# Three edits to a diffusion-transformer step: a conditioning vector partly summed on VectorE, squared relu on ScalarE, a low part computed one split later

## The chip, the core and the metric

The kernel runs on one core of a Trainium2 chip. Its time is the device time of one execution in microseconds (us). Five engines work side by side: TensorE (PE in the profile; PEld is its weight load), VectorE (DVE), ScalarE (ACT), GpSimd (POOL) and SyncE (SP). Here SP issues the loads of the layer weights, and POOL those of the conditioning weights. Engines wait for each other through semaphores, and each works through its own instructions in program order.

## The reference

Two layers of a transformer act on 128 context tokens and 128 latent tokens, 2048 wide. Each layer is modulated by six vectors per token kind, which come from a matrix product with the conditioning input:

```python
mod_ctx = (silu(c_ctx) @ w_ada[l] + b_ada[l])[None, None, :]
mod_lat = (silu(c) @ w_ada[l] + b_ada[l])[:, None, :]
shift1, scale1, gate1, shift2, scale2, gate2 = split(mod, 6)
h = rms_norm(x, g_attn) * (1 + scale1) + shift1
mix = concat(conv_module, global attention, windowed attention)(h @ w_in) @ w_out
x = x + gate1 * mix
h2 = rms_norm(x, g_mlp) * (1 + scale2) + shift2
x = x + gate2 * (square(relu(h2 @ w_mlp1)) @ w_mlp2)
```

w_ada[l] is 2048 x 12288, w_mlp1 2048 x 8192, w_mlp2 8192 x 2048, all float32. At the end both streams are normalised and written, with the keys and values of the context.

## The kernel before

**Pairs, halves, chunks.** Both token kinds lie side by side as 256 columns. A layer is 7 pairs of input projection, 4 of output projection, and 4 chunks c of the MLP with 4 "up" and 4 "down" pairs each. A pair makes 512 output rows in two halves g, each of which fills two PSUM banks from 16 blocks of 128 weight rows. A half is cut into four chunks h of four blocks. TensorE's `pair` (L705) does per block two matmuls of 512 columns with the weight's high part (L727) and two of 256 with its low part (L730).

**The split of the weights.** A weight is written as a rounded high part and the remainder. Per chunk ScalarE's `split_hi` (L965) makes the high part from the raw block, and VectorE's `split_lo` (L1298) the difference. There are four slots of each, so the split of chunk o waits until TensorE has finished chunk o - 4, and in each half both engines go through splits 4g+3 to 4g+6, that is three ahead. I call them splits 3, 4, 5 and 6 for either half. SP loads the raw blocks into four slots.

**The end of a half.** ScalarE copies the low products to `tmp` (`copies`, L1059), VectorE adds the banks to `tsum` (`both_summed`, L1481). In an up half VectorE squares the relu into `thid` (L1443), ScalarE rounds that into `act2` (L1044), and VectorE writes the low part (L1446). Only then does each engine come to the next half's split 3, VectorE to its `split_lo` and ScalarE to its `split_hi`, in this order of program. In a down half VectorE adds four pieces to `xT` (L1500). The next down pairs read `act2`, chunk h from the tiles 4h to 4h + 3; TensorE waits for them by `act2_ready`.

**The conditioning vectors.** Vectors are numbered v = 6 * layer + position. A vector is 16 row blocks k of `w_ada` (128 x 2048, 1 MB each). A unit is one block: four matmuls of 512 columns into four strips of a PSUM bank (`ada_products`, L605). POOL loads the blocks into five slots, `ring`: two in `ada`, two in `ring_q`, one in `thin`. Units stand in TensorE's stream behind chunk h = 2, as `units_inside` (L353) says: vector 4 two a half in the output pairs; vector 5 two behind norm 2, two in the second half of c = 0, then four in every second half, from four slots in turn; vector 6 one a half in c = 1, from slots 1 and 4.

Vectors 7 and 8 are folded instead: VectorE multiplies half a block (128 x 1024, `fold_in`, the slot 0) by the conditioning value of either token kind and adds it to `fold` (`fold_step`, L1463, L1474 for the first block and L1478 for the others), so a load is two steps. At the end TensorE sums the 128 rows of each kind with two units (`fold_sum`, L611). `fold_plan` (L1752) says which half does which loads: none in c = 0 up, then one a half, two in some, and two in every second down half. A fold step stands behind a split's low part. There are two buffers of half a block; POOL issues load n + 2 when both steps of load n are done, and issues a half's fold loads ahead of its unit load.

Of the kernel before, what the change touches and what calls it, by code (L numbers as in the profile page):

```python
# [11 lines left out]
S = 2  # L12
# [37 lines left out]
WIDE_VECTORS = (5, 11)  # L50
THIN_VECTOR = 6
FOLDED = (7, 8)
FOLD_LOADS = 2 * KT
FOLD_STEPS = FOLD_LOADS * S
# [47 lines left out]
def build(nc, t):  # L102
# [124 lines left out]
    relu2_ready, hid_hi = sem("relu2_ready"), sem("hid_hi")  # L227
# [90 lines left out]
    def unit_slot(v, k):  # L318


        if v == THIN_VECTOR:
            return (1, 4)[k % 2]
        if v in WIDE_VECTORS:
            return (k + 2 * (v == WIDE_VECTORS[0])) % 4
        return (0, 1, 4)[k % 3]

    def units_of(v):

        return S if v in FOLDED else KT
# [5 lines left out]
    def slot_uses(v, k):  # L335


        return [(w, j) for w in range(PRE_JOBS // 4, v + 1) if w not in FOLDED for j in range(KT if w < v else k)
                if unit_slot(w, j) == unit_slot(v, k)]
# [95 lines left out]
    with block:  # L435
# [64 lines left out]
        def _(pool):  # L500
# [11 lines left out]
            def thin_load(k):  # L512
                slot = unit_slot(THIN_VECTOR, k)
                pool.wait_ge(ada_used, slot_freed(THIN_VECTOR, k))
                pool.dma_start(ring[slot], w_ada(THIN_VECTOR)[:, k, :]).then_inc(ada_landed[slot], 16)

            def fold_load(load):
                n, at_half = divmod(load, FOLD_LOADS)
                k, h = divmod(at_half, 2)
                if load < 2:  # L520
                    pool.wait_ge(ada_used, used_before(THIN_VECTOR))
                else:
                    pool.wait_ge(folded, S * (load - 1))
                pool.dma_start(fold_in[:, h, :], w_ada(FOLDED[n])[:, k, h * (D // 2):(h + 1) * (D // 2)])\
# [23 lines left out]
            for v in range(PRE_JOBS // 4, THIN_VECTOR):  # L548
                vector(v // VECTORS, v)
            for load in range(2):  # L550
                fold_load(load)
            for k in range(2):
                thin_load(k)
            for c in range(CHUNKS):
                for kind in ("up", "down"):
                    for i in range(UP):
                        for g in range(2):
                            for load in FOLD_AT.get((c, kind, i, g), ()):
                                if load + 2 < FOLD_LOADS * len(FOLDED):
                                    fold_load(load + 2)  # L560
                            if c == 1 and half_of(kind, i, g) + 2 < KT:
                                thin_load(half_of(kind, i, g) + 2)
            pool.wait_ge(folded, FOLD_STEPS * len(FOLDED))
# [5 lines left out]
        def _(pe):  # L569
# [24 lines left out]
            def ada_unit(l, m, k):  # L594
# [4 lines left out]
                if v in FOLDED:  # L599
                    fold_sum(v, k)  # L600
                    return
                pe.wait_ge(ada_landed[unit_slot(v, k)], 16 * units_landed(v, k))
                ada_products(k, ring[unit_slot(v, k)])

            def ada_products(k, unit):  # L605
# [1233 lines left out]
```

## Time and profile before

| | us |
|---|---|
| median of 3 runs | 2247.67 (2246.96 to 2249.29) |
| the profiled execution | 2247.72 |
| its span, first to last instruction | 2245.9 |
| TensorE busy | 2200.5 |
| VectorE busy | 1523.4 |
| ScalarE busy | 1081.0 |

Busy times are sums over the whole span, and they do not tell which engine sets the pace of a stage; that is to be read from the timeline of the stage. A row of a timeline is the start, the duration, the engine and line, the operation, and in brackets how long the engine was idle before it and what it waited for. The bracket is left out where there was no idle time.

### The profile page before, as it was taken

How to read it: one execution, taken by the hardware profiler on the slowest of the kernel's cores; microseconds unless marked ns; L12 is line 12 of the kernel's file. 1: busy time of each engine (PE TensorE's matmuls, PEld its weight loads, DVE VectorE, ACT ScalarE, POOL GpSimd, SP SyncE). 2: the span in 40 equal slices, each digit the busy share in tenths (PEclk: the TensorE clock that was granted, in tenths of full speed). 3: DMA queues.
4: the chain of work that ended last, by engine and by line, in shares of the span. 5: the costliest groups of instructions: out<-in, count | busy, mean ns of one | idle time of the engine just before them, and what ended most of it. 6: DMA issues, size and time to landing. Idle time of an engine off the chain costs nothing.

```text
span 2245.9 us, 33331 instructions
## 1 busy us (share of the span) xinstructions
PE 2200.5 (98%) x13310; PEld 1823.1 (81%) x13310; DVE 1523.4 (68%) x2218; ACT 1081.0 (48%) x1566; POOL 112.4 (5%) x217
## 2 busy tenths in 40 slices
PE   6899999999999999999999999999999999999998
PEld 3677787778887888888887787888788888888887
DVE  2378765757877868888867876675556656655665
ACT  2245664644444334444455557574344444444444
POOL 1000100000000100000000000000000000000000
PEclk8999999999999999999999999999999999999999
DMA  9998878888888977887767787568756565556652
GB/s 374 407 381 323 297 275 318 291 308 296 264 282 297 333 231 236 265 255 230 230 232 261 285 322 259 203 202 281 243 188 182 192 192 188 191 190 189 192 190 95
DMA packets 403145, 571.07 MB, mean 254 GB/s; under 512 B 10744, under 2 KB 356976, under 8 KB 386352
## 3 DMA queue, kind: packets, MB, share of 16 engines
q1 hardware_dynamic: 372368, 398.77, 53.6%
q0 software_dynamic: 28320, 168.08, 19.9%
q8 instruction: 106, 1.74, 0.3%
q10 hardware_dynamic: 2304, 2.10, 0.3%
q14 instruction: 47, 0.39, 0.0%
HBM read 565.76 MB, written 3.15 MB: 253 GB/s over the span
## 4 chain that ended last, share of the span: by engine, by line
PE 94%; SPq 2%; DMA 2%; DVE 2%; ACT 1%; issue 0%; ACTq 0%; DVEq 0%
PE bank L727 46%; PE bank L730 22%; PE bank L823 9%; PE bank L607 5%; PE bank L826 4%; SPq L452 1%; PE bank L653 1%; PE bank L763 1%; DMA ada<-in_w_ada 1%; DVE lo L1302 1%; DMA raw<-in_w_in 1%; PE bank L629 1%; PE bank L766 1%; PE bank L656 0%; ACT hi L970 0%; PE bank L922 0%
## 5 line engine op out<-in xcount | busy, mean ns | idle before, releaser
L1302 DVE TENSOR_TENSOR lo<-raw,hi 128x1024 fp32r<-128x1024 f32 x688 | 833.0, 1222 | 334.8 <-ACT hi L970 333.4
L970 ACT ACTIVATE hi<-raw 128x1024 fp32r<-128x1024 f32 x688 | 716.2, 1055 | 568.9 <-PE bank L730 430.2
L727 PE MATMUL bank<-act,hi 128*128 128x512 f32 x2304 | 725.5, 396 | 0.5 <-DVE tsum L1486 0.5
L727 PE MATMUL bank<-hs,hi 128*128 128x512 f32 x2048 | 646.9, 397 | 0.2
L730 PEld LDWEIGHTS bank<-act,lo 128*128 128x128 f32 x2304 | 432.8, 188 | 102.4
L730 PEld LDWEIGHTS bank<-hs,lo 128*128 128x128 f32 x2048 | 385.0, 188 | 91.1
L730 PE MATMUL bank<-act,lo 128*128 128x256 f32 x2304 | 452.7, 278 | 0.0
L730 PE MATMUL bank<-hs,lo 128*128 128x256 f32 x2048 | 402.6, 278 | 0.0
L727 PEld LDWEIGHTS bank<-act,hi 128*128 128x128 f32 x2304 | 350.7, 189 | 12.4 <-DVE lo L1302 6.7
L727 PEld LDWEIGHTS bank<-hs,hi 128*128 128x128 f32 x2048 | 311.8, 189 | 18.7 <-issue 17.2
L1061 ACT ACTIVATE tmp<-bank 128x512 f32<-128x512 f32 x164 | 98.0, 597 | 345.3 <-PE bank L730 274.4
L823 PE MATMUL bank<-hs,hi 128*128 128x512 f32 x768 | 247.4, 403 | 0.1
L1486 DVE TENSOR_TENSOR tsum<-bank,tmp 128x512 f32<-128x512 f32 x140 | 96.7, 690 | 193.5 <-ACT tmp L1061 193.4
L826 PEld LDWEIGHTS bank<-hs,lo 128*128 128x128 f32 x768 | 144.4, 188 | 34.2
L1478 DVE SCALAR_TENSOR_TENSOR ring_q<-ada,cT,ring_q 128x1024 f32<-128x1024 f32 x120 | 153.4, 1279 | 0.0
L826 PE MATMUL bank<-hs,lo 128*128 128x256 f32 x768 | 151.3, 278 | 0.0
L823 PEld LDWEIGHTS bank<-hs,hi 128*128 128x128 f32 x768 | 117.5, 189 | 14.8 <-issue 10.4
L1614 DVE SCALAR_TENSOR_TENSOR yconv<-hpad,vecs,yconv 128x256 f32<-128x256 f32 x240 | 100.5, 478 | 0.0
L1044 ACT ACTIVATE act<-thid 128x512 fp32r<-128x512 f32 x64 | 40.4, 631 | 110.2 <-DVE thid L1443 110.2
L1500 DVE SCALAR_TENSOR_TENSOR xT<-tsum,mods,xT 128x128 f32<-128x128 f32 x304 | 86.6, 347 | 2.7
L607 PE MATMUL bank<-ada,cT 128*32 128x512 f32 x632 | 82.6, 617 | 1.0 <-DVE mods L1309 1.0
L1446 DVE TENSOR_TENSOR act<-thid,act 128x512 fp32r<-128x512 f32 x64 | 44.4, 693 | 53.5 <-ACT act L1044 53.5
(190 smaller groups left out, 1374.9 us busy)
## 6 DMA issues: line engine op xcount, KB each, us to landing
raw<-in_w_mlp SPq DMA_DIRECT2D x256, 1024.0 KB, 5.8
ada<-in_w_ada POOLq DMA_DIRECT2D x79, 1024.0 KB, 7.5
raw<-in_w_in SPq DMA_DIRECT2D x56, 1024.0 KB, 6.5
thin<-in_w_ada POOLq DMA_DIRECT2D x33, 1024.0 KB, 7.2
raw<-in_w_out SPq DMA_DIRECT2D x32, 1024.0 KB, 5.4
ada<-in_w_ada POOLq DMA_DIRECT2D x64, 512.0 KB, 4.3
pre_a<-in_w_ada SPq DMA_DIRECT2D x32, 512.0 KB, 10.8
ring_q<-in_w_ada POOLq DMA_DIRECT2D x16, 1024.0 KB, 9.8
```

Of the source, the lines that this page charges most:

```text
L607: mm = pe.matmul(ada_ps[32 * q:32 * q + 32, :], cT[:, k, :], unit[:, q * 512:(q + 1) * 512], start=(k == 0), stop=(k == KT - 1))
L727: pe.matmul(pb[2 * g + j][:, :], hi[:, h, k, j * P:(j + 1) * P], acts[:, k_, :], start=(k_ == 0), stop=False)
L730: mm = pe.matmul(pb[2 * g + j][:, TOK:2 * TOK], lo[:, h, k, j * P:(j + 1) * P], acts[:, k_, 0:TOK], start=False, stop=(k_ == KT - 1))
L823: pe.matmul(pb[2 * g + j][:, :], hi[:, slot, k, j * P:(j + 1) * P], acts[:, 4 * x + k, :], start=start, stop=False)
L826: mm = pe.matmul(pb[2 * g + j][:, TOK:2 * TOK], lo[:, slot, k, j * P:(j + 1) * P], acts[:, 4 * x + k, 0:TOK], start=False, stop=stop)
L970: act.activation(hi[:, o % 4, :, :], raw_chunk(n, o, s, sub), ACT.Copy).then_inc(hi_ready, 1)
L1061: act.activation(tmp[:, :, :], psum[:, 2 * g:2 * g + 2, TOK:2 * TOK], ACT.Copy).then_inc(tmp_ready, 2)
L1302: dve.tensor_tensor(lo[:, o % 4, :, :], raw_chunk(n, o, s, sub), hi[:, o % 4, :, :].bitcast(f32), ALU.subtract).then_inc(lo_ready, 1)
L1478: dve.scalar_tensor_tensor(fold[:, s, cols], fold_in[:, h, :], cT[:, k, s:s + 1], fold[:, s, cols], ALU.mult, ALU.add).then_inc(folded, 1)
L1486: dve.tensor_tensor(tsum[:, :, :], psum[:, 2 * g:2 * g + 2, 0:TOK], tmp[:, :, :], ALU.add)\
L1500: dve.scalar_tensor_tensor(x, total[:, :, s * P:(s + 1) * P], mods[:, l, bass.ds(gate + 4 * i + 2 * g + j, 1), s], x, ALU.mult, ALU.add).t ...
L1614: dve.scalar_tensor_tensor(y, hpad[:, ch, :, tap:tap + P], vecs[:, l, 1, 4 * tap + ch:4 * tap + ch + 1], y, ALU.mult, ALU.add).then_inc(co ...
```

## The change

- Vector 5 (`UP_VECTOR`) is done in pairs of units, in each up half of c = 0 but the first, from the slots 1 and 4 alone.
- Vector 6 (`SHARED_VECTOR`): blocks 0 to 7 stay units, in pairs in halves 8, 9, 11 and 12; blocks 8 to 15 are folded by VectorE in halves 1 to 7 and summed by two units in half 10.
- Vectors 7 and 8 are folded in halves 11 to 34 and 36 to 59, one load a half and two in every third.
- In an up half ScalarE does the relu, from `tsum` to `tmp`, and the square, from `tmp` to `thid`; VectorE's product is gone, and its next sum waits until the relu has read `tsum`.
- The low part of the squared relu is written by `hidden_lo`, in the next half, behind split 3 and the fold steps of that place.
- POOL's order in a half: that half's fold loads, then two unit loads.

```diff
+UP_VECTOR = 5
+SHARED_VECTOR = 6
+SHARED_TILES = 8
+FOLD_FIRST = {6: SHARED_TILES, 7: 0, 8: 0}
...
-        if v == THIN_VECTOR:
+        if v in (UP_VECTOR, SHARED_VECTOR):
             return (1, 4)[k % 2]
...
     def units_of(v):
-        return S if v in FOLDED else KT
+        return S if v in FOLDED else SHARED_TILES + S if v == SHARED_VECTOR else KT
+
+    def summed_part(v, k):
+        if v in FOLDED:
+            return k
+        return k - SHARED_UNITS if v == SHARED_VECTOR and SHARED_UNITS <= k < SHARED_UNITS + S else None
...
+        if a is not None and l == 0:
+            return [(a // 4, 4 * i + 2 * g + u) for u in range(0 if follows_norm(kind, i, c) and g == 0 else 2)]
         if a is not None and g == 1:
             return [(a // 4, 4 * i + u) for u in range(2 if follows_norm(kind, i, c) else 0, 4)]
-        if l == 0 and c == 1:
-            return [(THIN_VECTOR, half_of(kind, i, g))]
-        if l == 0 and (c, kind, i, g) in FOLD_SUMS:
-            return [(FOLD_SUMS[c, kind, i, g], s) for s in range(S)]
+        half = 2 * UP * 2 * c + half_of(kind, i, g)
+        if l == 0 and 0 <= half - SHARED_AT < (SHARED_TILES + S) // 2:
+            return [(SHARED_VECTOR, 2 * (half - SHARED_AT) + u) for u in range(2)]
+        if l == 0 and half in FOLD_SUMS:
+            return [(FOLD_SUMS[half], s) for s in range(S)]
...
+    def half_before(l, kind, i, c, g):
+        if g or i:
+            return kind, i - (g == 0), c, 1 - g
+        return ("up", UP - 1, c, 1) if kind == "down" else ("down", DOWN - 1, c - 1, 1)
...
+            ahead = [(UP_VECTOR, k) for k in range(2, KT)]
+            ahead += [(SHARED_VECTOR, k) for k in range(SHARED_TILES + S) if summed_part(SHARED_VECTOR, k) is None]
+            for half in range(4 * UP * CHUNKS):
+                for load in FOLD_AT.get(half, ()):
+                    if load + 2 < len(FOLD_PLACE):
+                        fold_load(load + 2)
+                for u in range(2):
+                    if ahead:
+                        unit_load(*ahead.pop(0))
...
                         if kind == "up":
                             first = 4 * i + 2 * g
+                            act.wait_ge(bank_freed, 4 * n + 2 * g + 2 - sums_left_out(l, kind))
+                            act.activation(tmp[:, :, :], tsum[:, :, :], ACT.Relu).then_inc(rectified, 2)
+                            act.wait_ge(rectified, up_tiles(l, c) + first + 2)
+                            if first:
+                                act.wait_ge(act2_ready, hidden_base(l, c) + first)
+                            act.activation(thid[:, :, :], tmp[:, :, :], ACT.Square).then_inc(relu2_ready, 2)
                             act.wait_ge(relu2_ready, up_tiles(l, c) + first + 2)
                             act.activation(act2[:, first:first + 2, 0:TOK], thid[:, :, :], ACT.Copy).then_inc(hid_hi, 2)
...
                                 split_lo(n, o)
-                            if l == 0 and (o - 4 * g - 3) // S < len(FOLD_AT.get((c, kind, i, g), ())):
-                                fold_step(FOLD_AT[c, kind, i, g][(o - 4 * g - 3) // S], (o - 4 * g - 3) % S)
+                            if l == 0 and kind != "out":
+                                for load, s in fold_steps(4 * UP * c + half_of(kind, i, g), o - 4 * g - 3):
+                                    fold_step(load, s)
+                            if o == 4 * g + 3:
+                                hidden_lo(*half_before(l, kind, i, c, g))
...
-                        if kind == "up":
-                            dve.scalar_tensor_tensor(thid[:, :, :], tsum[:, :, :], 0.0, tsum[:, :, :],
-                                                     ALU.max, ALU.mult).then_inc(relu2_ready, 2)
-                            dve.wait_ge(hid_hi, up_tiles(l, c) + first + 2)
-                            dve.tensor_tensor(act2[:, first:first + 2, TOK:2 * TOK], thid[:, :, :],
-                                              act2[:, first:first + 2, 0:TOK].bitcast(f32), ALU.subtract)\
-                               .then_inc(act2_ready, 2)
...
+                def hidden_lo(kind, i, c, g, l=l):
+                    if kind == "up":
+                        first = 4 * i + 2 * g
+                        dve.wait_ge(hid_hi, up_tiles(l, c) + first + 2)
+                        dve.tensor_tensor(act2[:, first:first + 2, TOK:2 * TOK], thid[:, :, :],
+                                          act2[:, first:first + 2, 0:TOK].bitcast(f32), ALU.subtract)\
+                           .then_inc(act2_ready, 2)
...
+                    if rectified_before:
+                        dve.wait_ge(rectified, rectified_before)
...
 def fold_plan():
+    at = {1: 3, 2: 3}
+    at.update({half: 2 for half in range(3, 8)})
+    for half in range(11, 35):
+        at[half] = 2 if half % 3 == 2 else 1
+    for half in range(36, 60):
+        at[half] = 2 if half % 3 == 0 else 1
     plan, first = {}, 0
+    for half in sorted(at):
+        plan[half] = range(first, first + at[half])
+        first += at[half]
...
+def fold_steps(half, position):
+    steps = [(load, s) for load in FOLD_AT.get(half, ()) for s in range(S)]
+    return steps[position::4] if len(steps) < 4 else steps[position * len(steps) // 4:(position + 1) * len(steps) // 4]
...
+FOLD_SUMS = {35: FOLDED[0], 61: FOLDED[1]}
```

In the diff halves are numbered through layer 0: 16c + position, up halves before down halves.

## Rows read from the trace of the kernel before

**Rows 1.** The page: TensorE's busy time, and the chain's shares by engine.
```profile
PE 2200.5 (98%) x13310; PEld 1823.1 (81%) x13310; DVE 1523.4 (68%) x2218; ACT 1081.0 (48%) x1566; POOL 112.4 (5%) x217
...
PE 94%; SPq 2%; DMA 2%; DVE 2%; ACT 1%; issue 0%; ACTq 0%; DVEq 0%
```

**Rows 2.** TensorE's waits: engine, line, awaited work, us in total, times, longest.
```profile
PE bank L653 <- DVE lo L1302: 6.0, 1, 6.0
```

**Rows 3.** Timeline of POOL: start, us, engine, line, operation, idle time before.
```profile
359.63 0.53 POOL L510 DMA_DIRECT2D ada<-in_w_ada  x1 [11.83 <-PE bank L607]
...
372.85 0.53 POOL L510 DMA_DIRECT2D thin<-in_w_ada  x1 [11.83 <-PE bank L607]
...
651.01 0.53 POOL L524 DMA_DIRECT2D ada<-in_w_ada  x1 [11.16 <-DVE ring_q L1478]
...
663.35 0.53 POOL L524 DMA_DIRECT2D ada<-in_w_ada  x1 [11.16 <-DVE ring_q L1478]
...
1050.56 0.53 POOL L524 DMA_DIRECT2D ada<-in_w_ada  x1 [10.61 <-DVE ring_q L1478]
```

**Rows 4.** Pieces of the chain that ended last: start, us, what.
```profile
444.18 1.85 PE bank L607 x16
468.55 3.57 PE bank L607 x32
494.61 3.57 PE bank L607 x32
```

**Rows 5.** Timeline of VectorE, an up half and the half behind it.
```profile
716.79 0.69 DVE L1486 TENSOR_TENSOR tsum<-bank,tmp 128x512 f32<-128x512 f32 x1 [2.11 <-ACT tmp L1061]
717.60 0.69 DVE L1443 SCALAR_TENSOR_TENSOR thid<-tsum 128x512 f32<-128x512 f32 x1
...
720.00 1.23 DVE L1302 TENSOR_TENSOR lo<-raw,hi 128x1024 fp32r<-128x1024 f32 x1 [0.19 <-ACT hi L970]
721.14 1.28 DVE L1478 SCALAR_TENSOR_TENSOR ring_q<-ada,cT,ring_q 128x1024 f32<-128x1024 f32 x1
722.34 1.22 DVE L1302 TENSOR_TENSOR lo<-raw,hi 128x1024 fp32r<-128x1024 f32 x1
...
729.33 0.68 DVE L1486 TENSOR_TENSOR tsum<-bank,tmp 128x512 f32<-128x512 f32 x1
```

**Rows 6.** Timeline of VectorE, a fold step on a vector's first block.
```profile
833.97 0.75 DVE L1474 TENSOR_SCALAR ring_q<-ada,cT 128x1024 f32<-128x1024 f32 x1
```

**Rows 7.** Timeline of ScalarE, the same half, and two operations of a mixer.
```profile
164.70 0.62 ACT L1215 ACTIVATE qsq<-zq 128x512 f32<-128x512 f32 x1
165.35 0.72 ACT L1220 ACTIVATE zq<-zq,vecs 128x512 f32<-128x512 f32 x1
...
716.10 0.60 ACT L1061 ACTIVATE tmp<-bank 128x512 f32<-128x512 f32 x1 [2.91 <-PE bank L730]
718.38 0.63 ACT L1044 ACTIVATE act<-thid 128x512 fp32r<-128x512 f32 x1 [1.69 <-DVE thid L1443]
718.92 1.99 ACT L970 ACTIVATE hi<-raw 128x1024 fp32r<-128x1024 f32 x2
```

**Rows 8.** Four loads in a row, issue to landing; and what the queues moved then.
```profile
DMA to landing us min/median/max: 6.9/9.8/12.9
...
DMA packets 364, 2.43 MB, mean 404 GB/s; under 512 B 32, under 2 KB 73, under 8 KB 73
```

**Rows 9.** Timeline of VectorE, the first up half's sum.
```profile
437.67 0.68 DVE L1486 TENSOR_TENSOR tsum<-bank,tmp 128x512 f32<-128x512 f32 x1
```

**Rows 10.** DMA issues of the page: the fold loads, median us to landing.
```profile
ada<-in_w_ada POOLq DMA_DIRECT2D x64, 512.0 KB, 4.3
```

**Rows 11.** Stretches: busy us of each engine, granted clock, DMA share, GB/s.
```profile
1180.00:1184.00 4.00, 3.02 (x16) 2.05 (x20) 2.11 (x5) 0.85 (x4) 0.00 (x0) 0.58 0.58 195
1184.00:1187.00 3.00, 3.00 (x17) 0.68 (x10) 3.00 (x12) 3.00 (x11) 0.56 (x2) 0.50 0.86 250
```

**Rows 12.** ScalarE's groups by form: table loads at the line of exp.
```profile
L1249 ACT ACT_TABLE_LOAD x6 | 7.7, 1283 | 0.1
```

More of the change, by code:

```diff
@@ L335, in slot_uses @@
     def slot_uses(v, k):
-        return [(w, j) for w in range(PRE_JOBS // 4, v + 1) if w not in FOLDED for j in range(KT if w < v else k)
-                if unit_slot(w, j) == unit_slot(v, k)]
+        return [(w, j) for w in range(PRE_JOBS // 4, v + 1) for j in range(units_of(w) if w < v else k)
+                if summed_part(w, j) is None and unit_slot(w, j) == unit_slot(v, k)]
     def slot_freed(v, k):
@@ L547, in _ @@
                          t["sink"].rearrange("l h -> (l h)").partition_broadcast(P)).then_inc(sinks_in, 16)
-            for v in range(PRE_JOBS // 4, THIN_VECTOR):
+            for v in range(PRE_JOBS // 4, UP_VECTOR):
                 vector(v // VECTORS, v)
+            for k in range(2):
+                unit_load(UP_VECTOR, k)
             for load in range(2):
                 fold_load(load)
[L552 to L563, printed above, removed]
+            ahead = [(UP_VECTOR, k) for k in range(2, KT)]
[7 more added lines that the diff above has]
+                        unit_load(*ahead.pop(0))
+            pool.wait_ge(folded, S * len(FOLD_PLACE))
             for v in range(FOLDED[-1] + 1, DEPTH * VECTORS):
@@ L598, in ada_unit, with ada_products @@
                 v = l * VECTORS + m
[L599 to L605, printed above, removed]
-                for q in range(4):
-                    mm = pe.matmul(ada_ps[32 * q:32 * q + 32, :], cT[:, k, :], unit[:, q * 512:(q + 1) * 512],
-                                   start=(k == 0), stop=(k == KT - 1))
-                mm.then_inc(ada_used, 1)
-            def fold_sum(v, s):
-                pe.wait_ge(pick_set, 1 + S)
-                pe.wait_ge(folded, FOLD_STEPS * (FOLDED.index(v) + 1))
-                for q in range(4):
-                    mm = pe.matmul(ada_ps[32 * q:32 * q + 32, :], pick[:, s, :], fold[:, s, q * 512:(q + 1) * 512],
-                                   start=(s == 0), stop=(s == S - 1))
+                s = summed_part(v, k)
+                if s is None:
+                    pe.wait_ge(ada_landed[unit_slot(v, k)], 16 * units_landed(v, k))
+                    ada_products(v, k, cT[:, block_of(v, k), :], ring[unit_slot(v, k)])
+                else:
+                    pe.wait_ge(pick_set, 1 + S)
+                    pe.wait_ge(folded, S * FOLD_END[v])
+                    ada_products(v, k, pick[:, s, :], fold[:, s, :])
+            def ada_products(v, k, weights, unit):
+                for q in range(4):
+                    mm = pe.matmul(ada_ps[32 * q:32 * q + 32, :], weights, unit[:, q * 512:(q + 1) * 512],
+                                   start=(k == 0), stop=(k == units_of(v) - 1))
                 mm.then_inc(ada_used, 1)
@@ L1531, in mixers @@
                     for g in range(2):
-                        both_summed("out", n, g)
+                        both_summed("out", n, g, up_tiles(l, 0))
                         for j in range(2):
@@ L1749, in half_of @@
     return 2 * UP * (kind == "down") + 2 * i + g
+FOLD_PLACE = [(v, k, h) for v in (SHARED_VECTOR,) + FOLDED for k in range(FOLD_FIRST[v], KT) for h in range(2)]
+FOLD_END = {v: max(load for load, place in enumerate(FOLD_PLACE) if place[0] == v) + 1 for v in (SHARED_VECTOR,) + FOLDED}
+SHARED_AT, SHARED_UNITS = 8, 4
 def fold_plan():
-    plan, first = {}, 0
-    for c in range(CHUNKS):
-        for kind in ("up", "down"):
-            for half in range(2 * UP):
-                i, g = divmod(half, 2)
-                loads = 1 + (kind == "down" and c < CHUNKS - 1 and g == 0)
-                if kind == "up" and (c == 0 or c == 2 and half < 2):
-                    loads = 2 * g * (c == 2)
-                if kind == "down" and c == CHUNKS - 1 and i > 1:
-                    loads = 0
-                if loads:
-                    plan[c, kind, i, g] = range(first, first + loads)
-                first += loads
-    assert first == FOLD_LOADS * len(FOLDED)
-    return plan
+    at = {1: 3, 2: 3}
[4 more added lines that the diff above has]
+        at[half] = 2 if half % 3 == 0 else 1
+    plan, first = {}, 0
+    for half in sorted(at):
+        plan[half] = range(first, first + at[half])
+        first += at[half]
+    assert first == len(FOLD_PLACE)
+    return plan
+def fold_steps(half, position):
+    steps = [(load, s) for load in FOLD_AT.get(half, ()) for s in range(S)]
+    return steps[position::4] if len(steps) < 4 else steps[position * len(steps) // 4:(position + 1) * len(steps) // 4]
 FOLD_AT = fold_plan()
-FOLD_SUMS = {(2, "up", 0, 0): FOLDED[0], (3, "down", 2, 0): FOLDED[1]}
+FOLD_SUMS = {35: FOLDED[0], 61: FOLDED[1]}
 HEAD_GROUPS = (0, 1, 2, 3, 4, 5, 6, 8, 10)
```

48 lines of the change are left out of this document (23 added, 25 removed).

## The prediction

> **What bounds the kernel now.** I read the page's busy shares first, then the chain of waits, then TensorE's own waits. TensorE is busy 98% of the span, and the chain that ends last runs through it for 94% [rows 1]. Its longest wait for VectorE is one of 6.0 us in the opening [rows 2]; in the multi-layer-perceptron part (MLP) its halves of a weight pair keep the length that their matmuls need (below). So two things count: how much TensorE has to do, and whether VectorE, which writes the low parts that TensorE waits for, still keeps up.
>
> I count in halves: half h = 16c + position, 0 to 63 in layer 0; 0-7, 16-23, 32-39 and 48-55 are "up" halves. A half has four chunks (0 to 3) of 2.79 us; vector units stand between chunk 2 and chunk 3. POOL's issues give the period: 0.53 + 10.61 = 11.14 us with no unit (11.15 in what follows), 12.34 with one, 13.22 with two [rows 3]. Two pieces of the chain, four units and then a half with none, lie 26.06 apart [rows 4]: minus 2 x 11.15, four units cost 3.76. So one costs 1.19, two 2.07, four 3.76: 0.86 each and 0.33 per interruption.
>
> **What goes from TensorE.** Before: vector 5 inside the up halves is 1 x 2 and 3 x 4 units, 2.07 + 11.28 = 13.35 us; vector 6 is 16 single ones, 19.04; together 32.4. After: seven pairs and five pairs (the two sums of the folded rows count as units), 12 x 2.07 = 24.8. Saved: 7.6 us, all on the path. The sums move from halves 32 and 60 to 35 and 61 at the same price.
>
> **What VectorE gets.** 16 more loads of half a block, two fold steps each: 32 steps in halves 1 to 7; later vectors are spread anew, with two loads (4 steps) in every third half instead of in "down" halves. The question is how long VectorE needs for one up half when it runs late. The trace has such a half: from one tsum at 716.79 to the next at 729.33, with four fold steps and no idle time before the second, 12.54 us [rows 5]. A fold step adds 1.20 to it (721.14 to 722.34). The first block of a vector is a plain multiply, 0.75 instead of 1.28 long [rows 6]: 0.53 less.
>
> Now the edits of the relu. Before, from tsum's start to the low part of split 3 is 720.00 - 716.79 = 3.21 us, and two VectorE operations of 0.69 stand in it. After, ScalarE does relu, square and copy there, and its split 3 is queued behind the copy, by its program order; so VectorE can do nothing until all of it is through. Price: tsum 0.69, release 0.09 (thid ends 718.29, ScalarE starts 718.38), relu 0.62 and its wait 0.03 (164.70 to 165.35, a square of the same size and the next operation, which waits for it), square 0.65, then 0.54 from the copy's start to the split's, and 1.08 to the low part [rows 5, 7]: 3.70. The deferred low part adds 0.61 behind it (its spacing, 0.69 less the overlap). Cycle with four steps: 12.54 - 3.21 + 3.70 + 0.61 = 13.65; with two 11.25, with six 16.05, with none 8.85. Against it TensorE's half: 11.15, or 13.2 with a pair of units. So each 4-step half puts VectorE 2.5 us further behind where there are no units, and 0.45 where there are. The move to ScalarE takes 0.7 us of work from VectorE and gives 3.1 us of idle time: it makes the cycle 1.1 longer. The bounds of the 3.70: 3.2 (ScalarE as fast as VectorE's own chain was) and 4.3 (each of three waits 0.2). In layer 1, with no fold steps, 8.85 is under 11.15 and costs nothing. At a change from up to down, TensorE's chunk 3 needs the deferred part: ready 0.8 + 5.6 = 6.4 us into the half with no steps, needed at 8.36; hidden, 2 us of cover.
>
> The Trainium skill ("ScalarE: Activation LUTs", Rules for kernel authors) says to put relu on VectorE. The trace agrees that it is the dearer place: 0.69 against 2 x 0.62 and a wait of 0.03, 0.6 more. Taken as a loss in each of the 64 up halves that would be 38 us, and 2278; by the rows it costs only where VectorE is late, and the sum below goes by that.
>
> **When TensorE stops.** Let S be the start of a half's first tsum (0.8 after the last half's end E if VectorE is on time: 716.10 for tmp, 716.79 for tsum [rows 5, 7]) and B = S + cycle. Then E >= S + 5.0 + 2.8 (low part of split 3, then chunk 3), the next chunk 0 not before S + 7.9, and the next S = max(E + 0.8, B). In a half behind the last up half, E >= S + 9.6 (deferred part). VectorE may be some 2.3 us late for free.
> c=1, halves 16 to 24, steps 2,4,2,2,4,2,2,4,2, from E = 0: S = 0.8, 12.05, 25.7, 36.95, 48.2, 61.85, 73.1, 84.35, 98.0; E of the last 107.6 against 9 x 11.15 = 100.35: 7.2 us of stalls, mostly in 21 (2.4) and 24 (4.2).
> c=2, 32 to 40: half 35 has no steps and two units, and lets VectorE catch up; 36 has cheap first steps (11.5). E 104.9 against 102.4: 2.5.
> c=3, 48 to 56, steps 4,2,2,4,2,2,4,2,2: again 7.2.
> Sum 16.9. With both ends of the 3.70 the cycle moves by -0.5 or +0.6 a half: 9 and 29.
>
> **The pairs of units in c=0.** POOL issues the two loads of the next pair behind the last fold load of the half, and that waits for the half's last fold step, at B. Vector 5 has now only two buffers, so nothing is ahead. Four loads in a row landed 6.9 to 12.9 us after their issues, 0.53 apart: the first after 6.9, each further one (12.9 + 1.59 - 6.9)/3 = 2.5 later [rows 8]. So from the fold load: 0.53 + 6.9 + 2.5 = 9.9, then the second unit 0.86, restart 0.4, chunk 3 2.8: E = B(last half) + 14.0, or E + 13.2 if that is later. VectorE starts half 1 late already (437.67; the unit piece at 444.18 less three chunks puts the half's start at 435.8): S = 1.9 [rows 4, 9]. Half 1 has six steps, four of them cheap, and its third load lands 1.2 late (issued after the first one's second step, 4.3 to land [rows 10]).
> Halves 1 to 7: B = 17.0, 33.05, 46.7, 61.5, 75.15, 89.95, 103.6; E of 1 to 8 = 13.2, 31.0, 47.05, 60.7, 75.5, 89.15, 103.95, 117.6 against 8 x 13.2 = 105.6: 12.0 us. Bounds: loads that land 1 us sooner or later give 6 and 18. The bytes: 5.24 MB a half (raw 2.1, units 2.1, folds 1.05), in 13.2 us 397 GB/s, where the busiest stretch moved 404 [rows 8]; no slack, but no term of its own.
>
> **Clock.** After a stretch with TensorE busy 3.02 of 4 us the granted clock was 0.50 (the 1.2 GHz level) for 3 us [rows 11]. A stall of over 2 us may bring this on, 1.5 us each, some eight times; most fall where VectorE is the bound anyway. I take 2, ends 0 and 12.
>
> **Sum.** -7.6 + 16.9 + 12.0 + 2 = +23.3 on the profiled execution's 2247.7 us (span 2245.9, and 1.8 around it), which is the median of the runs shown: 2271.
>
> **Rivals.**
> A. All stalls stay hidden (VectorE's lag is taken up by the four-deep splits, the loads land in time): 2247.7 - 7.6 = 2240. For it: in the kernel before, a 4-step half after an up half cost nothing. Against it: its cycle was 12.54 beside 12.34, the new one 13.65 beside 11.15. Chance 0.16.
> B. Only the pairs' loads are late: a VectorE cycle of 12.4 gives B = E, so E grows by 14.0 a half, 0.8 x 7, and some 2 more in each 6-step half: about 9; 2247.7 - 7.6 + 9 = 2249, no change. For it: half 1 to 7 are the only place where a load has one half to land. Chance 0.10.
> C. The loads land in time and VectorE alone holds: then c=0 costs 4 (chunk 3 >= S + 5 with S = 33.05 in half 3, slowly more to half 8), 2247.7 - 7.6 + 4 + 16.9 = 2261. Chance 0.12. It is inside my range.
> D. Relu and copy don't share ScalarE's tables: a load of 1.28 [rows 12] before and after, in each of 64 up halves. On the 24 folding ones of c=1 to 3 that is 2.6 us each, some 60 us on top: 2330. Against it: the trace has loads at the lines of exp, sqrt and sigmoid, and none between a square and a copy. Chance 0.02. The Trainium skill ("ScalarE: Activation LUTs", Table sets: the hidden batching unit) says that relu and copy are in every set; by that rule D cannot be, and the sum stays.
> The forecast itself 0.60, own range 2255 to 2284.
>
> **How the numbers follow.** What a measurement here can tell from no change is 0.2%, 4.5 us. Faster: A, 0.16. Within: B, 0.10. Slower: forecast, C and D, 0.74. The range goes from 2246 (leaves A out) to 2284 (bounds of the three costs, not all at once).
>
> **What would show it.** Right: tsum in the 4-step halves with no idle time before it, VectorE idle about 3.1 us before the low part of split 3 in each up half, TensorE waiting for the low part in halves 18 to 24 and 49 to 56 and for ada or thin in 2 to 7; the vectors' 128x512 matmuls down from 1040 to 1016. Wrong: VectorE idle before tsum in halves 20 and 23, or POOL's pair loads issued before the half's end in c=0. If TensorE's waits in the MLP are under 5 us in all, rival A holds.

## The result, and the profile after

The changed kernel takes 2285.3 us (median of 4 runs, 2280.9 to 2288.1) against 2247.7 of the kernel before (4 runs, 2247.0 to 2249.3): ratio 1.0165, 95% interval 1.0153 to 1.0177. It is slower, as forecast, but by 37.6 us where 23.3 were forecast, and 1.3 us above the range. The profiled execution is the fastest of the four: 2280.9, span 2279.1.

The page after. TensorE has 48 instructions fewer than in [rows 1] (six units, 8 records each) and yet 7.7 us more busy time; its share of the chain fell from 94% to 86%.

```profile
PE 2208.2 (97%) x13262; PEld 1829.1 (80%) x13262; DVE 1504.9 (66%) x2186; ACT 1158.3 (51%) x1694; POOL 117.1 (5%) x225
...
PE 86%; DMA 4%; DVE 4%; issue 2%; ACT 2%; SPq 2%; POOL 0%; ACTq 0%; DVEq 0%
```

TensorE's waits between 430 and 1240 us (awaited work, us in total, times, longest). Beside the 6.0 of [rows 2], which lies in the opening and is still there, the kernel before had none of the first four:

```profile
PE bank L737 <- DVE act L1499: 7.0, 3, 3.3
PE bank L627 <- DMA ada<-in_w_ada: 6.2, 3, 3.5
PE bank L627 <- DMA thin<-in_w_ada: 6.1, 5, 1.7
PE bank L737 <- DVE lo L1318: 5.9, 4, 2.3
PE bank L596 <- ACT thid L1083: 0.9, 2, 0.6
```

VectorE's timeline after, an up half with two fold steps (from the first sum to the second) and one with four; it answers to [rows 5].

```profile
686.64 0.68 DVE L1510 TENSOR_TENSOR tsum<-bank,tmp 128x512 f32<-128x512 f32 x1
690.54 1.23 DVE L1318 TENSOR_TENSOR lo<-raw,hi 128x1024 fp32r<-128x1024 f32 x1 [3.22 <-ACT hi L980]
...
692.88 0.69 DVE L1499 TENSOR_TENSOR act<-thid,act 128x512 fp32r<-128x512 f32 x1
...
698.09 0.69 DVE L1510 TENSOR_TENSOR tsum<-bank,tmp 128x512 f32<-128x512 f32 x1
701.99 1.23 DVE L1318 TENSOR_TENSOR lo<-raw,hi 128x1024 fp32r<-128x1024 f32 x1 [3.22 <-ACT hi L980]
...
711.93 0.68 DVE L1510 TENSOR_TENSOR tsum<-bank,tmp 128x512 f32<-128x512 f32 x1
```

No idle time stands before the sums: VectorE is the bound, with 11.45 us from sum to sum (686.64 to 698.09) and 13.84 (to 711.93). In both VectorE sits idle for 3.22 us behind its sum, until ScalarE's high part is there: 3.90 us from the sum's start to the low part. Why is in ScalarE's timeline of the same place; it answers to [rows 7].

```profile
698.87 0.63 ACT L1054 ACTIVATE tmp<-tsum 128x512 f32<-128x512 f32 x1 [3.30 <-DVE tsum L1510]
699.58 0.63 ACT L1058 ACTIVATE thid<-tmp 128x512 f32<-128x512 f32 x1
700.31 0.63 ACT L1060 ACTIVATE act<-thid 128x512 fp32r<-128x512 f32 x1
700.85 3.89 ACT L980 ACTIVATE hi<-raw 128x1024 fp32r<-128x1024 f32 x4
```

In chunk 0 of the MLP the pairs' loads come first. TensorE in half 2 waits for both; the two loads were issued behind the fold load of 453.90 (POOL's timeline, then TensorE's):

```profile
453.90 0.53 POOL L541 DMA_DIRECT2D ada<-in_w_ada  x1 [4.76 <-issue]
454.42 0.53 POOL L533 DMA_DIRECT2D ada<-in_w_ada  x1
454.94 0.53 POOL L533 DMA_DIRECT2D thin<-in_w_ada  x1
```

```profile
460.79 1.94 PE L627 MATMUL bank<-ada,cT 128*32 128x512 f32 x8 [3.53 <-DMA ada<-in_w_ada]
463.46 1.94 PE L627 MATMUL bank<-thin,cT 128*32 128x512 f32 x8 [0.74 <-DMA thin<-in_w_ada]
465.33 1.22 PE L737 MATMUL bank<-hs,hi 128*128 128x512 f32 x2
```

A unit takes 1.94 there, where at 480.29 it takes 1.07. The reason is the granted clock (third number from the end of a row; the same view as [rows 11]), at the 1.2 GHz level from 460 to 468:

```profile
456.00:460.00 4.00, 1.26 (x8) 0.92 (x6) 3.81 (x4) 2.94 (x4) 0.00 (x0) 0.91 1.01 414
460.00:464.00 4.00, 2.48 (x12) 0.40 (x16) 4.00 (x5) 0.00 (x0) 0.53 (x1) 0.50 0.97 347
464.00:468.00 4.00, 4.00 (x16) 2.29 (x9) 2.21 (x2) 0.00 (x0) 0.53 (x1) 0.50 0.99 334
```

ScalarE's table loads are those of [rows 12], at exp, sqrt and sigmoid, and none at the relu:

```profile
L1265 ACT ACT_TABLE_LOAD x6 | 7.7, 1283 | 0.1
```

**Where the time went.** I compare the profiles by ScalarE's first operation at the end of each half (`tmp`), in four stretches, one for each chunk c: halves 1 to 8, 16 to 24, 32 to 40 and 47 to 56. They take 106.55, 100.32, 103.28 and 111.46 us when TensorE never stops (back_best, the last version of the table below; what lies between the stretches is equal to 0.3 us in all kernels with the new plan). The table gives the excess over these, the excess of halves 1 to 62 as a whole ("sum", so up to 0.3 beyond its four columns), and TensorE's idle time there in waits of over 0.25 us:

| kernel | median us | c=0 | c=1 | c=2 | c=3 | sum | idle |
|---|---|---|---|---|---|---|---|
| after | 2285.3 | 19.9 | 10.6 | 3.3 | 7.1 | 40.8 | 25.2 |
| relu_back | 2257.5 | 11.2 | 0 | 0 | 0 | 11.2 | 7.7 |
| units_first | 2277.7 | 11.1 | 11.4 | 4.6 | 7.0 | 34.4 | 20.3 |
| hi_first | 2253.2 | 8.0 | 0 | 0 | 0 | 8.0 | 4.7 |
| no_relu | 2266.7 | 16.5 | 4.5 | 1.2 | 1.6 | 23.7 | 16.5 |
| slots | 2282.0 | 16.6 | 11.3 | 5.7 | 7.0 | 40.9 | 27.2 |
| best | 2241.2 | 0.5 | 0 | 0 | 0 | 0.5 | 0 |
| best_no_hi | 2267.5 | 5.4 | 10.5 | 3.3 | 7.0 | 26.2 | 17.6 |
| best_folds_first | 2243.4 | 7.7 | 0 | 0 | 0 | 7.7 | 5.1 |
| best_no_even | 2252.7 | 13.3 | 0 | 0 | 0 | 13.3 | 8.6 |
| back_best | 2240.4 | 0 | 0 | 0 | 0 | 0 | 0 |

From the end of half 0 to that of half 62 the kernel before takes 731.2 us, back_best 723.6: the 7.6 of the forecast. With 40.8 on top the changed kernel is at 764.4, 33.2 more than before, and so is its profiled execution (2280.9 against 2247.7). The columns say that idle time is not all: 40.8 us were lost to 25.2 of it.

### The profile page after: what moved, and what is told of

It is laid out like the page before. It is cut to its first block, busy times and chain, and to the rows that moved or that the text cites. A ratio compares the mean times of both kernels' runs of the same rounds, so it can differ in the third digit from the quotient of the medians.

```text
span 2279.1 us, 33485 instructions
## 1 busy us (share of the span) xinstructions
PE 2208.2 (97%) x13262; PEld 1829.1 (80%) x13262; DVE 1504.9 (66%) x2186; ACT 1158.3 (51%) x1694; POOL 117.1 (5%) x225
## 4 chain that ended last, share of the span: by engine, by line
PE 86%; DMA 4%; DVE 4%; issue 2%; ACT 2%; SPq 2%; POOL 0%; ACTq 0%; DVEq 0%
PE bank L737 41%; PE bank L740 20%; PE bank L833 9%; PE bank L627 5%; PE bank L836 4%; DMA thin<-in_w_ada 2%; DVE lo L1318 2%; SPq L470 2%; DVE ring_q L1491 1%; DMA ada<-in_w_ada 1%; DMA raw<-in_w_in 1%; PE bank L773 1%; ACT hi L980 1%; PE bank L663 1%; PE bank L776 1%
## 5 line engine op out<-in xcount | busy, mean ns | idle before, releaser
L1491 DVE SCALAR_TENSOR_TENSOR ring_q<-ada,cT,ring_q 128x1024 f32<-128x1024 f32 x148 | 189.2, 1280 | 6.7 <-DMA ada<-in_w_ada 6.7
L1054 ACT ACTIVATE tmp<-tsum 128x512 f32<-128x512 f32 x64 | 40.5, 633 | 102.0 <-DVE tsum L1510 102.0
L541 POOL DMA_DIRECT2D ada<-in_w_ada x80 | 42.4, 530 | 621.7 <-DVE ring_q L1491 546.1
```

Of the source, the lines that this page charges most:

```text
L1491: dve.scalar_tensor_tensor(fold[:, s, cols], fold_in[:, h, :], cT[:, k, s:s + 1], fold[:, s, cols], ALU.mult, ALU.add).then_inc(folded, 1)
```

## The experiments

Beside them the kernel before took 2247.7 to 2248.7 us (medians). The diffs are shortened: dots stand for code left out, and long lines are abridged.

**relu_back.** The changed kernel with the three relu edits undone, loads and fold plan as changed.

```diff
-act.activation(tmp, tsum, ACT.Relu); act.activation(thid, tmp, ACT.Square)
-if o == 4 * g + 3: hidden_lo(*half_before(...))
+dve.scalar_tensor_tensor(thid, tsum, 0.0, tsum, ALU.max, ALU.mult); hidden_lo(kind, i, c, g)
```

> The changed kernel with the relu's three edits undone: relu and square in one VectorE operation, its low part at once, before the next half's split 3. The fold plan and the pairs stay. Theory 1 (VectorE's cycle of an up half grew to 13.8 us because it stands idle while ScalarE does relu, square and copy ahead of split 3): the cycle goes back to 12.5 with four steps and 10.2 with two, the stalls in c=1 to 3 (20.9 us in the changed kernel) vanish, those in c=0 (20.8) fall to about 11; 2252 to 2258. Theory 2 (it is the amount of VectorE's work in the up halves, 32 more fold steps, and the relu's edits relieve it): 0.7 us more work per up half, so no faster than 2285.

2257.5 (2254.0 to 2264.2), ratio 1.005 (1.0034 to 1.0065). All stalls of c=1 to 3 are gone. c=0 keeps 11.2 us: 7.7 us of waits, all for loads, and the rest behind them, most of it at the 1.2 GHz level in half 2. So the three relu edits together cost 28 us of the 38.

**relu_only.** The other half: the kernel before with the three relu edits, its own vectors and fold plan.

> The kernel before with the three edits of the relu alone (relu and square on ScalarE, low part behind split 3); its fold plan, thin units and groups of four stay. Theory 1: a cycle with two steps is 11.45 against TensorE's 11.15 in c=2 and c=3 up, so the lag grows by 0.3 a half and ends in a stall of 1.5 to 2 us at the change to down, twice: 2250 to 2252, slower by 0.1 to 0.2%. Theory 2 (less work for VectorE is a relief): 2247 or faster, and no stall.

2253.0 (2250.6 to 2254.1), ratio 1.0021 (1.0012 to 1.003), 1 us above what the first theory gave. The edits alone cost 5 us, in two places (halves 40 and 56, behind the last up half of c=2 and c=3):

```profile
PE bank L733 <- DVE act L1493: 3.5, 2, 2.0
```

5 us alone and 28 with the new fold plan: they matter by what VectorE still has to do in up halves. The kernel before has no fold step in those of c=0 and two in most of the others; the changed one has four or six in c=0, and elsewhere four in every third half and two in the rest.

**units_first.** The changed kernel, POOL issuing the two unit loads of a half ahead of its fold loads.

```diff
 for half in range(4 * UP * CHUNKS):
+    for u in range(2): ... unit_load(*ahead.pop(0))
     for load in FOLD_AT.get(half, ()): ... fold_load(load + 2)
-    for u in range(2): ... unit_load(*ahead.pop(0))
```

> The changed kernel with one order turned: in each half POOL issues the two unit loads ahead of that half's fold loads, so they wait for TensorE's units and no longer for VectorE's last fold step. Theory 1: the waits of TensorE for ada and thin in halves 2 to 8 vanish, the lag of VectorE stays; c=0 stalls fall from 20.8 to 5 to 9, the rest stays: 2269 to 2275. Theory 3 (the transfers themselves are the bound in c=0, 397 GB/s asked of 404): no gain, 2283 or more.

2277.7 (2273.6 to 2282.9), ratio 1.0132 (1.0114 to 1.0151), above the 2269 to 2275 of the first theory and below the 2283 of the other. No wait for ada or thin is left in the MLP of layer 0, so the transfers do fit. VectorE's lag takes over in c=0: six waits for `lo`, 7.2 us, where the changed kernel had none, and 11.1 us of excess where 5 to 9 were expected. Two limits lay there on top of each other.

**hi_first.** The changed kernel, ScalarE making the high part of split 3 ahead of the relu. All else on ScalarE and VectorE stays.

```diff
+ahead = o == 4 * g + 3 and half_before(l, kind, i, c, g)[0] == "up"
+if not (last and o >= 8 or o == 3 and follows_norm(kind, i, c) or ahead): split_hi(n, o)
 ...
 first = 4 * i + 2 * g
+split_hi(*((n + 1, 3) if g else (n, 7)))
 act.wait_ge(bank_freed, ...)
 act.activation(tmp[:, :, :], tsum[:, :, :], ACT.Relu).then_inc(rectified, 2)
```

> The changed kernel with ScalarE's order turned in an up half: the high part of the next half's split 3 comes right behind the copy of tmp, ahead of relu, square and copy. All the work stays on its engine. Theory 1: VectorE's idle 3.2 us before split 3's low part goes, the cycle is about 10.9 with four steps and 13.4 with six, under TensorE's half; stalls in c=1 to 3 vanish (-20.9), those in c=0 fall to 5 to 8: 2248 to 2254. Theory 2 (the amount of work): nothing changes, 2285.

2253.2 (2247.4 to 2257.1), ratio 1.0023 (1.0013 to 1.0032). One instruction three places further ahead in its queue removes all stalls of c=1 to 3. Here is VectorE with it, in the best version below, at a place like that of the timeline above:

```profile
687.48 0.69 DVE L1517 TENSOR_TENSOR tsum<-bank,tmp 128x512 f32<-128x512 f32 x1
688.43 1.23 DVE L1325 TENSOR_TENSOR lo<-raw,hi 128x1024 fp32r<-128x1024 f32 x1 [0.27 <-ACT hi L985]
...
698.62 0.69 DVE L1517 TENSOR_TENSOR tsum<-bank,tmp 128x512 f32<-128x512 f32 x1 [1.14 <-ACT tmp L1084]
```

0.27 us of idle time behind the sum instead of 3.22, and now the sum waits for `tmp`, i.e. for TensorE.

**no_relu.** The changed kernel without the relu; ScalarE's chain is one operation shorter, the order stays.

> The changed kernel without the relu itself: ScalarE squares tsum directly, so its chain between tsum and its high part of split 3 is one operation (0.71 us) shorter; everything else, order and loads included, stays. It leaves the relu out of the computation. T1 (the length of ScalarE's chain sets VectorE's cycle, and the cycle sets the stalls): cycle of a 4-step up half 13.1 instead of 13.84, of a 2-step one 10.7 instead of 11.45. By the same recursion as in the prediction the last up half of chunks 1 and 3 then ends 3.5 us late instead of 7.2; measured with the slow clock behind it, chunks 1 to 3 should lose 7 to 12 us together instead of 20.8, chunk 0 (halves 0 to 8) 3 to 6 less than the 20.8 of the changed kernel. Time 2266 to 2273. T2 (not the length but the crossing of queues costs, ScalarE's high parts behind anything of VectorE's): the stalls stay above 17 us in chunks 1 to 3, time over 2278.

2266.7 (2262.6 to 2269.5), ratio 1.0087 (1.0072 to 1.0102). The cycle of a 4-step half is 13.11 (692.17 to 705.28), and c=1 to 3 lose 7.3 us instead of 20.9: both as worked out from the length of the chain. 0.7 us off each cycle is worth 18.6 us of the whole, the slow clock behind the stalls included.

**slots.** The changed kernel with the first four units of vector 5 there before half 0 (the first two in the buffers 2 and 3).

> The changed kernel with vector 5's first four units already there at half 0: its first two go to ring buffers 2 and 3 (free since the mixers), the next two to buffers 1 and 4. T1 (the wait for thin at norm 2 and a part of the waits of half 2 come from only two buffers being ahead): no wait for thin before half 0, half 0 starts at 436 or before in each run (the changed kernel's median loses 2 to 4 us there, its profiled run 1.2), and half 2 (21.4 us with 8.2 of stall) gets 2 to 5 shorter; the VectorE part stays, 20.8 us in chunks 1 to 3. Time 2275 to 2281. T2 (half 2 is set by VectorE and the late fold load, not by the pair's loads): halves 0 to 8 stay within 1.5 us of 126.4; time 2281 to 2285.

2282.0 (2276.4 to 2283.2), ratio 1.0151 (1.0136 to 1.0166), 1 us above the first theory's 2275 to 2281. A wait of 1.2 us at norm 2 has gone, but half 2 is only 0.95 us shorter (20.42) where 2 to 5 were expected: two more buffers do not help while each pair is issued behind VectorE's last fold step. That wait I had not foreseen. The kernel before has four buffers there; in the changed one POOL sends vector 5's second unit only when `thin` is free of vector 4, at 412.32, and TensorE wants it at norm 2, ahead of half 0 (POOL's timeline, then TensorE's wait between 400 and 437 us):

```profile
412.32 0.53 POOL L533 DMA_DIRECT2D thin<-in_w_ada  x1 [11.54 <-PE bank L627]
```

```profile
PE bank L627 <- DMA thin<-in_w_ada: 1.2, 1, 1.2
```

It is 1.2 us in the profiled execution of the changed kernel, and 0.9, 2.2, 3.7 and 4.6 in those of no_relu, units_first, hi_first and relu_back, which run the same code up to that place. So it seems to vary from run to run; no kernel was profiled twice.

**best.** hi_first and units_first together, two fold loads in each of halves 1 to 8, and the buffers of slots.

```diff
-    at = {1: 3, 2: 3}
-    at.update({half: 2 for half in range(3, 8)})
+    at = {half: 2 for half in range(1, 9)}
```

> The changed kernel with four edits: ScalarE's high part of split 3 ahead of the relu; POOL issues a half's two unit loads ahead of its fold loads; two fold loads in each of halves 1 to 8 instead of three in 1 and 2; the first four units of vector 5 loaded before half 0. T1 (ScalarE's order, the load order and the two buffers are all that costs; the saving of 7.6 us by pairs is real): halves 0 to 8 in 105.6 to 108, chunks 1 to 3 at 100.35, 103.3 and 111.5, time 2238 to 2244, faster than both kernels. T2 (VectorE's four fold steps a half don't fit into the 13.2 us of a half with a pair, whatever the order): halves 0 to 8 stay over 112, time 2247 or more. T3 (the transfers don't fit, 397 GB/s asked for): waits for ada and thin over 5 us between halves 1 and 8, time over 2246.

2241.2 (2239.1 to 2241.8, 8 runs), ratio 0.997 (0.9959 to 0.998): faster than both. TensorE's waits of over 0.25 us in halves 1 to 62 are gone, at 382 GB/s between 440 and 560 us.

**back_best.** The same loads and plan with the relu on VectorE as before.

> The changed kernel with the relu back on VectorE in the order of the kernel before, and the three edits of the loads (unit loads ahead of fold loads, two fold loads in each of halves 1 to 8, the first four units of vector 5 loaded before half 0). T1 (pairs and folding are worth 7.6 us, and only their load order took it away): halves 0 to 8 in 105.6 to 108, time 2238 to 2244. Beside the version with ScalarE's relu and the high part ahead it tells what the relu's place is worth by itself: by T1 nothing, within 2 us. T2 (with VectorE's full load a 4-step half takes 12.54, under 13.2, but the relu on ScalarE is needed for slack): over 3 us slower than that version.

2240.4 (2239.1 to 2241.7, 8 runs), the same interval. The place of the relu is worth nothing by itself: all of the gain is the six units and eight interruptions (22 groups of units in halves 1 to 62 before, 14 after) that TensorE is spared.

**best_no_hi, best_folds_first, best_no_even.** One edit of the best version put back in each. The fourth, the buffers of slots, was not put back by itself.

> The best version (2241.2 us) with only its ScalarE order put back: high part of split 3 behind relu, square and copy again, the three load edits stay. T1 (that order alone sets VectorE's cycle of 13.84 in a 4-step half; loads are no part of it): chunks 1 to 3 lose 20 to 22 us again; in chunk 0, four steps in every half, the cycle is 0.6 over the 13.2 us of a half with a pair, seven halves, 4 us of lag of which 2 are free, and the last fold half passes into one with none: 2 to 7 us. Time 2263 to 2270. T2 (load order and ScalarE order each were a half of it): below 2255.

> The best version with only its load order put back: POOL issues a half's fold loads ahead of its two unit loads again. T1 (a pair behind the last fold load arrives about E + 13.2 or a little later, so TensorE waits a little in each of the halves 2 to 8; with VectorE on time B = E + 0 and 14.0 - 13.2 = 0.8 a half): halves 0 to 8 in 110 to 113 instead of 107.0, chunks 1 to 3 as in the best version, time 2243 to 2248. T2 (with four units ahead and VectorE on time the order is free): within 1 us of the best version.

> The best version with only the fold plan put back: three fold loads (six steps) in halves 1 and 2, two in 3 to 7, none in 8. T1 (a six-step half takes VectorE 2.4 us longer than the 13.2 of a half with a pair, twice, with the third load 1.2 late; about 2.3 us are free, so some 2 to 5 us are lost and with them perhaps 1.5 by the clock): halves 0 to 8 in 109 to 114, time 2243 to 2248. T2 (the splits ahead hide it): within 1 us of the best version.

2267.5, 2243.4 and 2252.7: ScalarE's order costs 26.3, the load order 2.2 and the uneven fold plan 11.5. The first two times came as worked out, though in the profiled execution of best_folds_first, at 2246.5 one of its slowest, halves 0 to 8 took 114.3 where at most 113 were expected. The third cost is two to five times what I expected, and the timelines of VectorE and POOL show why:

```profile
462.29 2.48 DVE L1498 SCALAR_TENSOR_TENSOR ring_q<-ada,cT,ring_q 128x1024 f32<-128x1024 f32 x2 [15.30 <-DMA ada<-in_w_ada]
464.69 0.68 DVE L1517 TENSOR_TENSOR tsum<-bank,tmp 128x512 f32<-128x512 f32 x1
```

```profile
445.50 0.53 POOL L538 DMA_DIRECT2D ada<-in_w_ada  x1 [30.63 <-PE bank L632]
446.48 0.53 POOL L538 DMA_DIRECT2D thin<-in_w_ada  x1 [0.46 <-PE bank L632]
448.15 1.05 POOL L546 DMA_DIRECT2D ada<-in_w_ada  x2 [1.14 <-issue]
```

The half's third fold load, the first of the two of 448.15, stands in POOL's queue behind the pair, which waits for TensorE's units until 445.50; its own buffer was free from about 443.4. The two half-size loads of 448.15 landed 14.5 us (median) after their issue, and VectorE, whose sum stands behind that fold step in its queue, was idle for 15.3 us. The pair itself took longer than in best, 13.0 and 14.5 us against 9.6 and 11.3; why is open. The pair first is right only where no fold step of the same half still needs a load.

**stall_dose.** What a stall costs, by itself: back_best, and in eight halves TensorE waits ahead of chunk 3 for POOL, which clears a free buffer.

```diff
+if half in DOSES:
+    pool.wait_ge(half_used, 8 * n + 4 * (half % 2) + 3)
+    for m in range(DOSES[half]): ... pool.memset(ring[4][:, 0:512], 0.0).then_inc(dosed, 1)
 ...
+if half in DOSES: pe.wait_ge(dosed, sum(DOSES[x] for x in DOSES if x <= half))
```

> The price of a stall of TensorE measured by itself: the version with VectorE's relu and the three load edits (no stalls of its own in chunks 1 to 3, 2240.4 us), and in eight halves of layer 0 (18, 22, 27, 30, 40, 44, 52, 56) TensorE waits ahead of chunk 3 for POOL, which clears a free buffer 2, 3, 4, 6, 5, 8, 12 and 1 times, one after the other, once chunk 2 is through. Nothing else waits for POOL. T1 (a stall costs its own length and then a stretch at the 1.2 GHz level): after waits of up to about 1 us the periods return at once (excess = wait); after waits of 1.5 us and more the granted clock falls to 0.50 for some us and the excess is 1 to 2.5 us more than the wait; in all the extra is what the changed kernel lost beyond my terms. T2 (a stall costs just its length; the extra us of the changed kernel came from its loads and queues): excess within 0.3 us of the wait in all eight, clock at 0.95 or more. If a clearing takes 0.5 us, the eight waits are 20 us and the time 2260 by T2, 2265 to 2273 by T1.

2293.9 (2 runs), far above both theories' times, 2260 and 2265 to 2273. POOL came to its clearings late, so the eight stalls were longer than planned, 2.5 to 9.7 us and 36.5 in all instead of 20. What they tell is read from each stall:

| half | 27 | 56 | 22 | 30 | 18 | 44 | 40 | 52 |
|---|---|---|---|---|---|---|---|---|
| TensorE idle, us | 2.48 | 2.53 | 3.54 | 3.64 | 4.20 | 4.80 | 5.59 | 9.67 |
| excess of the half and the next, us | 2.71 | 4.32 | 6.33 | 5.18 | 6.01 | 6.60 | 7.72 | 12.47 |
| difference | 0.2 | 1.8 | 2.8 | 1.5 | 1.8 | 1.8 | 2.1 | 2.8 |

TensorE's timeline after the first two of these stalls. The profile names VectorE's low part for the one of half 27, as that ended last (775.70), but POOL's last clearing ended at 775.61, 0.15 us before the matmul, and in half 56 it ended 0.14 before (1136.57), so this is the planned stall too.

```profile
775.76 0.70 PE L753 MATMUL bank<-act,hi 128*128 128x512 f32 x2 [2.48 <-DVE lo L1328]
776.53 0.63 PE L753 MATMUL bank<-act,hi 128*128 128x512 f32 x2
...
1136.71 1.14 PE L753 MATMUL bank<-act,hi 128*128 128x512 f32 x2 [2.53 <-POOL thin L590]
1138.08 1.05 PE L753 MATMUL bank<-act,hi 128*128 128x512 f32 x2
1139.37 1.00 PE L753 MATMUL bank<-act,hi 128*128 128x512 f32 x2
1140.44 0.63 PE L753 MATMUL bank<-act,hi 128*128 128x512 f32 x2
```

Two stalls of one length: after the one a pair of matmuls takes 0.63 at once, after the other 1.05 for some 3.5 us. After the one of half 18 the granted clock was:

```profile
664.00:667.00 3.00, 2.18 (x9) 1.92 (x10) 1.01 (x1) 0.00 (x0) 0.62 (x2) 0.79 0.90 286
667.00:669.00 2.00, 2.00 (x7) 1.61 (x7) 0.00 (x0) 0.00 (x0) 0.00 (x0) 0.50 0.99 323
669.00:672.00 3.00, 3.00 (x19) 2.65 (x18) 1.39 (x2) 0.81 (x2) 0.00 (x0) 0.98 0.09 30
```

So the first theory holds but for half 27, where it expected a slow stretch: a stall costs its length and then either 0.2 us, or 1.5 to 2.8 with a stretch at the 1.2 GHz level, and the second price hardly grows with the length (9.67 us of stall pays 2.8, as 3.54 does).

## Why the prediction missed, by its own steps

**What goes from TensorE (7.6): right.** From half 0 to half 62 it is 731.2 us before against 723.6 in back_best. The count of matmuls that I named as a sign was wrong: the vectors' groups go from 1056 to 1008 records, not from 1040 to 1016.

**VectorE's cycle: right in its cause, 0.2 short in size.** 13.65 and 11.25 were forecast, 13.84 and 11.45 measured. I spaced ScalarE's dependent operations 0.65 apart, as a square and the operation behind it in [rows 7]; relu, square and copy come 0.71 to 0.73 apart (698.87, 699.58, 700.31). Hence 3.90 instead of 3.70. hi_first and no_relu show the cause: the same operations in another order cost nothing, and a chain 0.7 shorter costs a third. Without the clock's part the lag costs 19.1 us where 16.9 were forecast: 8.8 in c=1, 7.0 in c=3 (both from slots, which had no slow clock in c=3 and one in c=1, whose 2.5 are taken off) and 3.3 in c=2.

**The pairs' loads in c=0 (12.0): right within the error.** The excess is 19.9. slots and no_relu, which kept the 2.4 GHz level in halves 4 and 6, had 16.6 and 16.5, so 3.3 of it are two slow stretches. Half 2 has another, 3.9 beyond its idle time; that leaves 12.7. This 3.9 rests on an argument: no kernel had waits of over 3 us in half 2 without a slow stretch. But one part of it I had put elsewhere: the pair came 11.1 us after VectorE's sum (452.30 to 463.4) instead of 9.9, and later halves less. And waits for loads were only the visible limit: units_first took them away, and VectorE's lag kept 11.1 us, 2.5 of them beyond the stall in a slow stretch of half 2.

**The clock (2, ends 0 and 12): this is the step that failed.** I had put it at eight stretches of 1.5 us and took only 2 of these 12, because "most fall where VectorE is the bound anyway". There were six slow stretches (halves 2, 4, 6, 21, 24, 55), each 1.6 to 3.9 us beyond the stall, 12.6 together, and of these 33.2 - (-7.6 + 19.1 + 12.7) = 9.0 us stayed in the time of the profiled execution. So price and number were near, and the share that another engine's lag absorbs was not. The 9.0 is what the other terms leave over, not a measurement of its own; stall_dose measured the price of a stretch. For the stalls in the midst of the up halves my reason holds: in c=3 half 55 had its slow stretch in the changed kernel (4.24 us of excess) and not in slots (2.70), and half 56 paid the rest in idle time, 0.59 against 1.95; both stretches end at 7.0 or 7.1. It does not hold for a stall at the end of VectorE's lag (half 24, 1.8 us) nor in c=0, where slow matmuls follow a wait for a load and the next pair is not nearer for it. My own bound of 12 held it; the value I took was near the other end. [Rows 11] I had read wrongly as well: there the clock fell within the first of the two stretches, at 1180.6, and stayed at the 1.2 GHz level for 6.8 us, not 3. Here is the stall of half 21, first in the changed kernel and then in slots, each with the stretch of 3 us that begins some 2 us behind it:

```profile
717.10 0.73 PE L737 MATMUL bank<-hs,hi 128*128 128x512 f32 x2 [2.25 <-DVE lo L1318]
719.00:722.00 3.00, 3.00 (x11) 2.51 (x10) 3.00 (x3) 0.57 (x1) 0.00 (x0) 0.50 0.90 282
```

```profile
714.10 0.73 PE L742 MATMUL bank<-hs,hi 128*128 128x512 f32 x2 [2.25 <-DVE lo L1323]
716.00:719.00 3.00, 3.00 (x18) 2.54 (x17) 3.00 (x3) 0.60 (x1) 0.41 (x1) 1.00 0.90 286
```

The Trainium skill ("TensorE: Matmul & The Clock Gate", Part 1: The HAM clock gate) says that the clock follows how busy the array was lately and has only two levels, and that the point at which it changes differs from run to run of one kernel. All fourteen traces agree on the levels: the granted clock is 0.50 or 1.00 in each of their records. On the last point they only fit: the stall of half 21, 2.25 us long in four kernels, brought 1.2 GHz in three and not in the fourth, but no kernel was profiled twice.

**The sum.** -7.6 + 19.1 + 12.7 + 9.0 = +33.2 for the profiled execution, against +23.3: +7.0 by the clock, +2.2 by the cycle, +0.7 by the loads. A last part is not in that execution: the median of the runs is 4.4 above it. The wait at norm 2, for which the forecast had no term (1.2 us there, 0.9 to 4.6 in the four other profiles named above), and stretches that are slow in one run and not in the next can make such a difference; slots, without that wait, has a median 3.3 lower. Which share is whose was not separated, so the cause of these 4.4 us, without which the median would have stayed inside the range, is open.

**The rivals.** A (all hidden) and B (only the loads) fall by the waits for `lo` and `act`. C held in part: VectorE alone costs c=0 some 11 us with its slow stretch, and 8.6 without, not 4 (units_first). D falls: no table load stands at the relu.

## What to carry to other kernels

Ask of every instruction that moves to another engine what is queued behind it there: the relu itself was free on either engine, but the high part behind it cost 26 us, and three places further ahead in the queue made it nothing. Load in the order in which the data are needed, and give work that shares a queue in equal portions, or the third load of one half stops two engines. And price a stall of TensorE as its own length plus what a stretch at the slow clock behind it may cost, 1.5 to 3.0 us in these traces, unless another engine's lag absorbs it.

## What the runs showed of the hardware

- Stalls of TensorE in layer 0's MLP that had no other stall within 8 us, counted over all profiled kernels (the granted clock fell within 5 us of their end, or during them): of those under 1.2 us none had the 1.2 GHz level behind it; of 1.3 to 2.0 us, 2 of 13; of 2.2 to 3.1 us, 10 of 16; of over 3.3 us, 11 of 11. Without it a stall cost at most 0.7 us beyond its length, with it 1.5 to 3.0.
- A 128x512 operation of ScalarE that waits for the one before it starts 0.71 to 0.73 us after it (duration 0.63); one that does not wait, 0.54 (700.31 to 700.85).
- POOL's 1 MB loads of half 1 landed 9.6 and 11.3 us after their issue in best, 13.0 and 14.5 in best_no_even, with the queues at 327 to 405 GB/s from 448 to 456 us; those of half 2 took 6.0 to 8.4. The half-size ones, 4.5 us by the page's median of the changed kernel, took 11.8 and 14.5 (medians of two) issued behind such a pair.
